# A decoder trunk on one core: stage boundaries in another order, norm factors as a row through memory, both parts of the step sizes in one product, and a later place for waits in the attention loop

## The reference, cut to what matters

```python
h += 0.5 * post_norm(SwiGLU_1(pre_norm(h)))           # d_ff 2816
h += post_norm(mixer_i(pre_norm(h)))                  # i = 0: hybrid, i = 1: latent attention
h += 0.5 * post_norm(SwiGLU_2(pre_norm(h)))
h += post_norm(sigmoid(pre_norm(h) W_g) * (p[i] W_p)) # "ple"
rmsnorm(x, g) = x * rsqrt(mean(x * x) + 1e-6) * g
# hybrid: gelu gating (8 groups of 128) beside a Mamba-2 scan
dt = softplus(dt + dt_bias)                           # 16 step sizes of each token
xd = x * dt[..., None]                                # scan input
y  = y + d_skip[:, None] * xs                         # skip
# latent attention: 16 heads, low-rank queries and keys, causal
```

## Time and profile before

| | |
|---|---|
| time, median of 3 runs | 1134.64 us (1133.79 to 1135.49) |
| the profiled execution | 1133.96 us, its span 1132.2 us |
| granted TensorE clock | 0.999 |
| PE busy | 1107.9 us, 98% |
| PEld busy | 935.3 us, 83% |
| DVE busy | 817.4 us, 72% |
| ACT busy | 565.5 us, 50% |
| POOL busy | 86.4 us, 8% |
| DMA | 207.83 MB, mean 184 GB/s |

### The profile page before, as it was taken

One profiled execution on the slowest core, in us unless ns is written; L12 is line 12 of the kernel. 1 busy time (PEld: TensorE's weight loads), 2 busy tenths in 40 slices (PEclk: granted clock), 3 DMA queues, 4 the chain that ended last, 5 costly groups with the idle time before them and its releaser, 6 DMA issues.

```text
span 1132.2 us, 14058 instructions
## 1 busy us (share of the span) xinstructions
PE 1107.9 (98%) x5713; PEld 935.3 (83%) x5713; DVE 817.4 (72%) x1053; ACT 565.5 (50%) x692; POOL 86.4 (8%) x124
## 2 busy tenths in 40 slices
PE   8999999999999999999999999999999999999997
PEld 5888888788788788888887888888888878888885
DVE  5867777588997677777775867767865667776774
ACT  7444444567464554444555544446655555444443
POOL 2000000201210200000022000001200020000012
PEclk9999999999999999999999999999999999999999
DMA  9555555645543565555565555554523365555541
GB/s 319 207 196 193 186 186 177 240 178 186 186 167 128 192 219 192 197 196 188 183 205 191 209 186 186 190 189 170 195 75 113 112 222 196 186 189 191 195 169 56
DMA packets 31168, 207.83 MB, mean 184 GB/s; under 512 B 3713, under 2 KB 3761, under 8 KB 7681
## 3 DMA queue, kind: packets, MB, share of 16 engines
q1 hardware_dynamic: 27648, 194.00, 48.2%
q0 software_dynamic: 3456, 12.94, 3.4%
HBM read 205.86 MB, written 1.06 MB: 183 GB/s over the span
## 4 chain that ended last, share of the span: by engine, by line
PE 62%; DVE 10%; ACT 3%; issue 2%; POOL 1%; DMA 0%; DVEq 0%; POOLq 0%; ACTq 0%
PE PS L604 17%; PE PS L189 10%; PE PS L191 10%; PE PS L190 10%; PE PS L607 9%; DVE WL L171 4%; ACT WH L164 1%; PE PS L371 1%; PE PS L1727 1%; PE PS L1726 1%; DVE hn L1336 1%; PE PS L1745 1%; PE PS L1735 0%; PE PS L1027 0%; DVE ca L1291 0%
## 5 line engine op out<-in xcount | busy, mean ns | idle before, releaser
L171 DVE TENSOR_TENSOR WL<-raw,WH 128x2048 fp32r<-128x2048 f32 x181 | 413.3, 2289 | 155.2 <-ACT WH L164 155.1
L164 ACT ACTIVATE WH<-raw 128x2048 fp32r<-128x2048 f32 x181 | 344.9, 1908 | 119.2 <-DMA raw<-stream 119.2
L604 PE MATMUL PS<-X,WH 128*128 128x512 f32 x1152 | 288.3, 392 | 0.0
L604 PEld LDWEIGHTS PS<-X,WH 128*128 128x128 f32 x1152 | 209.1, 189 | 38.8
L607 PEld LDWEIGHTS PS<-X,WL 128*128 128x128 f32 x1152 | 157.1, 190 | 11.3
L607 PE MATMUL PS<-X,WL 128*128 128x256 f32 x1152 | 160.6, 282 | 0.0
L189 PE MATMUL PS<-WH,X 128*128 128x512 f32 (+1 forms) x352 | 139.9, 397 | 7.7 <-DVE WL L171 5.8
L706 ACT ACTIVATE sgb<-sgb 128x256 f32<-128x256 f32 x72 | 30.1, 418 | 227.9 <-DVE sgb L702 227.9
L191 PE MATMUL PS<-WL,X 128*128 128x512 f32 (+1 forms) x352 | 136.9, 389 | 0.0
L190 PE MATMUL PS<-WH,X 128*128 128x512 f32 (+1 forms) x352 | 136.8, 389 | 0.0
L189 PE MATMUL PS<-WH,BH 128*128 128x512 f32 x288 | 113.1, 393 | 0.0
(11 more groups left out here) (274 smaller groups left out, 1313.3 us busy)
## 6 DMA issues: line engine op xcount, KB each, us to landing
raw<-stream SPq DMA_DIRECT2D x181, 1024.0 KB, 4.8
PG<-post_g POOLq DMA_DIRECT2D x8, 512.0 KB, 6.6
QG<-pre_g POOLq DMA_DIRECT2D x7, 512.0 KB, 7.3
raw<-stream SPq DMA_DIRECT2D x4, 512.0 KB, 8.1
Eg<-acs_rows POOLq DMA_DIRECT2D x2, 1024.0 KB, 6.1
h<-x SPq DMA_DIRECT2D x2, 512.0 KB, 5.8
out<-h SPq DMA_DIRECT2D x4, 256.0 KB, 2.1
wsT<-gm_w POOLq DMA_DIRECT2D x1, 512.0 KB, 9.2
```

The lines of the kernel that those rows point to most:

```text
L164: act.activation(WH[:, n % RING, :], raw[:, n % RING, :], ACT.Copy).then_inc(sem("w_hi"), 1)
L171: dve.tensor_tensor(WL[:, n % RING, :], raw[:, n % RING, :], WH[:, n % RING, :], ALU.subtract).then_inc(sem("w_lo"), 1)
L604: pe.matmul(PS[:, bank, :], wh[:, kt, cols], X[:, kt, :, :].rearrange("p a n -> p (a n)"), start=kt == 0, stop=False)
```

## The change

It has six parts.

1. Boundaries on VectorE and ScalarE. `split_to(m + 3)` moves between the two `x_low` of the second token half; `split_to(m + 2)` moves behind `post_mean` of the second half (after a `ple`, m + 2 stays and m + 3 has that place already). After a `ple`, ScalarE splits m + 3 between the sigmoids and the squares. VectorE takes `ple_product` and `gained` in turns.
2. The norm factors reach `rs_row` over memory: GpSimd writes the two columns to `rs_mem`, waits, and reads them back into all partitions. TensorE's and ScalarE's parts of it go.
3. The hybrid's step sizes: `dt_hi` and `dt_lo` lie side by side, 32 columns, and meet XH and XL as one operand of 512 columns, in 8 matmuls. The 32 x 512 result is copied and turned back by 4 matmuls with `both`, two identities on top of each other. The product of the two low parts, left out before, is thereby in the sum.
4. The skip moves to VectorE, into `times_dt`; `copy_xs` on ScalarE and `skip` on GpSimd go. Some of VectorE's steps in this stage stand in another order.
5. The attention loop: TensorE waits for the queries' emptying later in the round, ScalarE empties them before the exponentials of the odd head, and VectorE normalises the odd head before it splits.
6. The opening: x comes in four quarters, the first products are transposed for quarter by quarter, and ScalarE splits unit 2 before the second square.

```diff
-        def post_square(act, s, t):
+        def post_square(act, s, t, between=None):
             for b in range(2):
                 if stages[s][0] == "ple":
                     ple_sigmoid(act, s, t, b)
+            if between is not None:
+                between()
...
         def behind(dve, s, t, between=None):
-            if stages[s][0] == "ple":
-                ple_product(dve, s, t, 0)
-                ple_product(dve, s, t, 1)
             for b in range(2):
+                if stages[s][0] == "ple":
+                    ple_product(dve, s, t, b)
                 gained(dve, s, t, b)
...
-            post_square(act, s - 1, 1)
-            if stages[s - 1][0] == "ple":
-                split_to(m + 3)
+            post_square(act, s - 1, 1, (lambda: split_to(m + 3)) if stages[s - 1][0] == "ple" else None)
...
-        def opening_act(act, done):
+        def opening_act(act, done, split_to):
...
+            first_x_high(act, 1, 0)
             first_x_high(act, 0, 1)
-            first_x_high(act, 1, 0)
             first_part_hi(act, 1, 0)
             first_x_high(act, 1, 1)
             first_part_hi(act, 1, 1)
+            done[0] = 2
             pre_square(act, 0, 0)
+            split_to(2)
             pre_square(act, 0, 1)
             load_table(act, ACT.Silu)
-            done[0] = 2
...
             x_low(dve, s, 0, (1,))
-            if stages[s][0] != "mla":
-                split_to(m + 2)
-            behind(dve, s - 1, 1, (lambda: split_to(m + 3)) if from_ple else None)
             if stages[s][0] == "mla":
+                behind(dve, s - 1, 1)
                 x_low(dve, s, 1, (0,))
                 return
-            x_low(dve, s, 1)
+            if before == "ple":
+                split_to(m + 2)
+            behind(dve, s - 1, 1, lambda: split_to(m + 3 if before == "ple" else m + 2))
+            x_low(dve, s, 1, (0,))
             split_to(m + 3)
+            x_low(dve, s, 1, (1,))
...
                     if s == 0 and (j, t, q) == (0, 0, 2):
-                        transpose_x(pe, 0, 1)
+                        transpose_x(pe, 0, 1, (0,))
+                    if s == 0 and j == 0 and t == 1 and q % 2 == 0:
+                        transpose_x(pe, 0, q // 2, (1,))
...
-        def rs_row_pe(pe, s):
-            pe.wait_ge(sem("pre_rs"), 2 * s + 2)
-            for t in range(2):
-                ins = pe.matmul(PS[:, 6, tok(t)], col(s, t, RS).broadcast_to([P, P]), ident[:, :], start=True, stop=True)
-            ins.then_inc(sem("rs_tr"), 1)
...
-        def rs_row_act(act, f):
-            act.wait_ge(sem("rs_tr"), f + 1)
-            act.activation(rs_row[:, :], PS[:, 6, 0:SEQ], ACT.Copy).then_inc(sem("rs_there"), 1)
+        def rs_row_pool(pool, s, f):
+            pool.wait_ge(sem("pre_rs"), 2 * s + 2)
+            for t in range(2):
+                pool.dma_start(rs_mem[tok(t)].rearrange("(p n) -> p n", n=1), col(s, t, RS)).then_inc(sem("rs_out"), 16)
+            pool.wait_ge(sem("rs_out"), 32 * (f + 1))
+            pool.dma_start(rs_row[:, :], rs_mem.partition_broadcast(P)).then_inc(sem("rs_there"), 16)
...
             for kt in range(KT):
-                ins = product(pe, PS[0:HEADS, P1, 0:SEQ], dt_hi[:, kt, :], dt_lo[:, kt, :], XH[:, kt, :], XL[:, kt, :],
-                              kt == 0, kt == KT - 1)
+                ins = pe.matmul(PS[0:2 * HEADS, P1, :], dt_parts[:, kt, :, :].rearrange("p a h -> p (a h)"),
+                                X[:, kt, :, :].rearrange("p a n -> p (a n)"), start=kt == 0, stop=kt == KT - 1)
...
             for t in range(2):
-                ins = pe.transpose(PS[:, P1, t * HEADS:(t + 1) * HEADS], dtT[:, tok(t)], ident[0:HEADS, 0:HEADS])
+                for part in range(2):
+                    ins = pe.matmul(PS[:, P1, t * HEADS:(t + 1) * HEADS], dtT[:, part * SEQ + t * P:part * SEQ + (t + 1) * P],
+                                    both[:, :], start=part == 0, stop=part == 1)
...
             def times_dt(t):
-                dve.wait_ge(sem("hy_xs"), t + 1)
+                dve.wait_ge(sem("hy_back"), t + 1)
+                dve.tensor_tensor(heads(xs[:, t, :]), heads(flat_pair(CT)), per_head(DV, HEADS, 64), ALU.mult)\
+                   .then_inc(sem("hy_skip"), 1)
...
             normalise(0)
+            times_dt(1)
             split_to(u + 16)
-            times_dt(1)
             normalise(1)
...
-                if j == 1:
-                    wait_emptied(Q2)
-                if j == 2:
-                    wait_emptied(Q3)
                 transpose_probabilities(2 * j)
...
+                if j == 1:
+                    wait_emptied(Q2)
                 if 0 < j < 7:
                     out_unit(j - 1, 0)
...
+                if j == 2:
+                    wait_emptied(Q3)
                 if 1 < j < 7:
                     out_unit(j - 2, 1)
...
                 copy_pT(2 * j + 1)
+                if j < 2:
+                    take((Q2, Q3)[j])
                 if j < 7:
                     exponentials(2 * j + 3)
-                if j < 2:
-                    take((Q2, Q3)[j])
...
-                split_to(u + 7 + j)
+                if j:
+                    split_to(u + 7 + j)
                 if j < 7:
                     maxima(2 * j + 3)
                     normalise(2 * j + 3)
+                split_to(u + 7 + j)
```

More of the change, by code:

```diff
@@ L276, in h_ready @@
             else:
-                eng.wait_ge(sem(f"x_loaded{t}"), 16)
+                for b in range(2):
+                    eng.wait_ge(sem(f"x_in{t}{b}"), 16)
         def pre_square(act, s, t):
@@ L469, in opening_act @@
             first_part_hi(act, 1, 1)
+            done[0] = 2
             pre_square(act, 0, 0)
+            split_to(2)
             pre_square(act, 0, 1)
             load_table(act, ACT.Silu)
-            done[0] = 2
         def boundary_dve(dve, s, done, split_to):
             m = first[s] if s < NS else n_units
-            from_ple = stages[s - 1][0] == "ple"
-            split_to(m if from_ple else m + 1)
+            before = stages[s - 1][0]
+            split_to(m if before == "ple" else m + 1)
             behind(dve, s - 1, 0)
@@ L521, in boundary_pool @@
                 inverse_rms(pool, s, t)
+            if stages[s][0] == "ffn":
+                rs_row_pool(pool, s, stages[s][1])
         def load_gains(pool, s):
@@ L888, in hybrid_trunk @@
         Btok = place("Btok", [P, 2 * STATE], offset=o); o += 1024
+        both = place("both", [2 * HEADS, HEADS], offset=o); o += 64
         assert o <= end, o
@@ L1499, in hyb_pool @@
             pool.memset(cx[:, :, 0:3], 0.0).then_inc(sem("hy_pad"), 1)
+            pool.tensor_tensor(both[:, :], ident[0:2 * HEADS, 0:HEADS], ident[0:2 * HEADS, HEADS:2 * HEADS], ALU.add)\
+                .then_inc(sem("hy_both"), 1)
             pool.dma_start(gm_g[:, :], a["gm_g"].partition_broadcast(P)).then_inc(sem("hy_gm"), 16)
@@ L2121, in _ @@
             load_part(0, 1)
-            sp.dma_start(h[:, 1, :], a["x"][tok(1), :]).then_inc(sem("x_loaded1"), 16)
+            load_x(1, 0)
+            load_x(0, 1)
+            load_x(1, 1)
             load_part(1, 0)
@@ L2155, in _ @@
             done, split_to = splitter(act, split_hi)
-            opening_act(act, done)
+            opening_act(act, done, split_to)
             for s, (kind, _) in enumerate(stages):
```

63 lines of the change are left out of this document (27 added, 36 removed).

## The result

The changed kernel takes 1147.15 us (median of 6 runs, 1144.08 to 1151.49) against 1134.03 for the kernel before beside it (6 runs): a ratio of 1.0115, interval 1.0094 to 1.0135. It is slower, where I had forecast 1129.7. It lies near that of my rival (c), 1145.7, to which I gave 0.06. The profiled execution took 1146.47 us, its span is 1144.7 and its granted clock 0.994.

The account below looks back on a forecast made before the run. TensorE, busy 98% of the span at full clock, was taken to bound the kernel. The terms 4.05 + 1.45 + 1.0 - 1.85 + 0 + 0.3 = 4.95 us off gave 1129.7 us, range 1125.8 to 1132.2.

Parts of the forecast that it names:

- rival (c): At the `ffn` starts the row comes late and TensorE stands; 1145.7 us at a chain of 17 us; chance 0.06.
- the row over memory: Four times, norm factors go through memory on GpSimd's queue: chain 9 us, up to 13, cost 0.
- the 13 of cover: At the `ffn` after `ple`, some 13 us pass before TensorE notices a late row: 11.5 plus 1.5 to 2.
- The estimate by the Trainium skill: Row chain by about 2.0 us fixed and bytes over 436 GB/s: an estimated 6 us, with the sum the same.
- The boundaries: Reordered stage starts remove TensorE's waits on WL, gaining 4.05 us; the end of the last stage gains 0.3.
- The three starts: At `hyb`, the `ffn` after it and the `ffn` after `mla`, the wait on WL goes: 1.0 us each, 3.0.
- The price: GpSimd's power behind `post_mean` is held by VectorE's moved split, so `h` comes some 0.55 us after the split.
- Rival (b): Stage starts give half: the held power makes `hn` late at every start; -2, 1131.7 us; chance 0.15.
- The hybrid stage: VectorE bounds it; `normalise` without GpSimd's skip beside it, less added products, gains 1.0 us, ends 0 and 2.5.
- The loop of `mla`: TensorE waits for `CL` behind VectorE's later split: 0.95 and 0.9 us later in two rounds, a loss of 1.85.
- The opening: `x` in quarters, TensorE takes up unit 2 at 24.6 against 24.55: 0 us, ends -0.7 (loss) and +0.7.
- the 1.45 of the row's products: At four places two products leave TensorE, 0.36 us each record, 1.45 in all.

Follow-up runs that it names:

- e13: The changed kernel with each norm factor copied four times and written as a 16-byte piece, row still over memory: 1128.89 us, ratio 0.9956.
- e3: The changed kernel with the row of norm factors made by TensorE and ScalarE as in the kernel before: 1131.45 us, ratio 0.9973.

## Why the prediction was wrong

**The step that failed** is the row over memory: "I take 0.6 + 4 + 0.3 + 4 = 9, up to 13 with loads beside it", hence "Cost 0". The chain took 17.3 to 18.3 us and cost 16.7. The two 4's came from `acs_rows`, which is near by queue and by size but not by form: it writes 32 rows of 512 bytes, the new one 128 single numbers next to each other. The step said that no such transfer was in the trace, and then bounded it with 13, a number that no row gives. The far end that it named itself, 14.1 for one transfer, would have made the chain 19 us or more, over the 13 of cover. With that end kept, the range had to reach rival (c), and its 0.06 was far too little for a cost known from no row.

**Rival (c) itself** had the mechanism: a row that comes late stops VectorE and then TensorE. That its time, 1145.7, is within 1.5 us of the measured one is partly luck. "Each microsecond over 13 is one on the path, four times" held for the wait in the `ffn` after `ple`, where a chain of 18.33 less a wait of 5.08 leaves 13.2 of cover. In the other three the cover was 15.1 to 15.5, as the forecast's own "12 to 14 and the same reserve" allowed. So the waits are 11.9 us in all and not the 19 that the rule gives at the measured chains, and what the row cost beyond the waits, 4.8, the rival didn't have. "Against it: nothing is queued before it" was no argument: the reason isn't a queue before it, the write is slow by its form, 7.3 us in `mla` with one load beside it for a third of that time.

**The estimate by the Trainium skill**, "DMA: Bandwidth & Descriptors", "Anatomy of one DMA — SWDGE (gpsimd) path", 6 us for the chain, was further off than mine: even with pieces that hold nothing up the chain takes 10.8 to 11.4 us (`e13`). My 9, up to 13, would have held for that form.

**The boundaries** were right in sum: 4.35 forecast with the end, 4.7 measured (4.1 in the traces). The parts were not, and cancel. The three starts gained 1.2 each instead of 1.0, but that of `hyb` was lost again inside the stage, which my own reading of it, VectorE without a gap and TensorE waiting, should have told me. The `ffn` after `ple` gained 0.96 instead of 0.45, the first change from `ffn` to `ple` 0.1 instead of 0.3, and the last change with the end 1.0 instead of 0.6. The price was right: the power behind `post_mean` is held by VectorE's split of 202.54,

```profile
202.71 2.53 POOL L326 TENSOR_TENSOR stat<-stat,nhalf 128x1 f32<-128x1 f32 x1 [6.48 <-DVE stat L319]
```

2.53 us against 0.55, and the mean of the sixteen has gone from 554 to 1297 ns. The exclusive lock between VectorE and GpSimd that the Trainium skill states, "SBUF — State Buffer", "SBUF: two separate sides", agrees with it. What the forecast didn't see is that the meeting moved more than it was added: before, it was `inverse_rms` (L293, L298) that met the splits, and its two operations have gone from 31.8 to 20.9 us in all while the powers went from 8.9 to 20.7. Rival (b), that this makes `hn` late everywhere, did not come: each of the three starts gained 1.2.

**The hybrid stage**: 1.0 forecast, 1.5 measured. The account by VectorE held: in the changed kernel a run of eight `normalise` operations takes 2.19 us beside nothing on GpSimd, against 3.84.

**The loop of `mla`**: sign and mechanism right, the size not: -1.85 forecast, -3.4 in the trace. The term was mis-sized by the clock, 1.6 us. (The 0.26 us that the prediction takes as the distance of two starts is a little too much: it divides a time that holds the last record's whole length. The starts lie 0.23 apart. No term changes by it.)

**The opening**: 0 forecast, a loss by both pairs of runs, of 0.4 to 1.6 us; whether it lies outside the end of 0.7 that I gave it is open.

**The sum without the row.** My terms without the 1.45 of the row's products give 3.5; `e3` measured 2.7 (1134.14 - 1131.45). That is the same verdict as the forecast's; the row alone turned it. The nearness is partly luck: the hybrid stage gave more than I had taken, the loop and the opening cost more.

## What to carry to other kernels

A transfer whose form is not in the trace has no price: bound it by the worst row of its queue, and compare forms by how their pieces lie in memory, not by bytes. Do not write single numbers from many partitions next to each other; 16 bytes for each, or 64 bytes of distance, took 4.5 us where they took 10. An operation that leaves TensorE for a queue saves what it took there, here 0.36 to 0.5 us, and stakes every microsecond by which the queue comes late; here the chain took twice the length that I had reckoned, 17.8 against 9. A start that is made quicker pays only where the stage behind it is bound by the engine that starts sooner. And where a split is moved behind something that waits, look at what stands behind the split.

## What the runs showed of the hardware

- 128 single float32 numbers written next to each other in memory took 10.0 and 10.6 us beside a stream of weights, and 7.3 in a place where one load was under way for the first 2.3 us; 64 or 1024 bytes apart, in 16-byte pieces, or into the core's own memory, 4.5 to 4.6.
- While they are under way, the DMA engines count as busy and move almost nothing: 33 to 43 GB/s where 395 went before. A load of 1 MB that met one took 9.6 to 9.8 us beside the steady stream, where its neighbours took 4.8, and 10.5 instead of 6.2 in the second `ffn`. So one small transfer on GpSimd's queue slows SyncE's large ones.
- Two such writes issued together had landed after 10.2 to 11.7 us, issued 3.9 to 4.8 us apart after 18.9 to 20.5.
- A power on GpSimd took 2.53 us when a VectorE split of 2.28 us had just begun, 0.55 otherwise.
- Behind TensorE's waits for the row of 2.36 and 5.08 us the granted clock fell to 0.63 and 0.59 on the mean of four microseconds; behind those of 2.14 and 2.28 it stayed at 1.00. The changed kernel's times go with the clock of the run: from 1144.08 at 0.996 to 1151.49 at 0.991.
